# Layer norms of the residual tails: sums and squares of uncentred tiles as they come, then two tiles normed per group, with all low parts of u on one engine

## The chip, the cores and the metric

One core of one Trainium2 chip runs the whole program. The metric is the device time in microseconds, the median over runs. PE is TensorE, DVE VectorE, ACT ScalarE, POOL GpSimd, SP SyncE.

## The reference, cut to what matters

Two transformer blocks over 512 tokens of width 1024, then two layers of another block. Each of the two first layers has three residuals, and each residual ends in a layer norm whose result goes, modulated, into the next product:

```python
def layer_norm(x, g, b):
    mu = jnp.mean(xf, -1, keepdims=True)
    var = jnp.mean(jnp.square(xf - mu), -1, keepdims=True)
    return ((xf - mu) * lax.rsqrt(var + LN_EPS) * g + b)

def deepnorm_residual(x, f, gate, g, b, weight=1.0):
    return layer_norm(DN_ALPHA * x + weight * (1 + gate) * f, g, b)

for l in range(DEPTH):          # DEPTH = 2
    x = deepnorm_residual(x, swiglu(modulate(x, sh1, sc1), ...), g1, ..., 0.5)
    x = deepnorm_residual(x, mixer(modulate(x, sh2, sc2)), g2, ...)
    x = deepnorm_residual(x, swiglu(modulate(x, sh3, sc3), ...), g3, ..., 0.5)
```

## The kernel before

Activations lie transposed, as eight tiles of 128 features by 512 tokens (XA). A product walks over its output tiles m; for each, PE multiplies k = 8 or 11 weight tiles. Each fp32 product is made of three matmuls: high part of the weights by high and low part of the input, low part of the weights by the high part (L560 to L562).

Weights come as slabs of at most 1024 columns through a ring of three raw buffers (SP loads them) and a ring of three split buffers. ACT writes the high part (L481, `act_slabs`), then DVE or POOL the low part (L491, `low_slabs`). The letters of `low_in` and `low_out` name the engine, by the slab's number modulo their count: v is DVE, g is POOL. A slab with k = 8 is one tile of 1024 columns; a tile with k = 11 has two slabs of 768 and 640 columns. A split buffer is free once PE has ended the tile that used it.

Every engine has one queue, in the order in which its program (a generator) emits. `act_linear`, `dve_linear` and `pool_linear` do the same for each m: first the slabs up to `L.ahead(m)` (with one slab a tile: up to tile m + 2; with two: up to both slabs of tile m + 1), then the epilogue of m. `pe_linear` calls `after(m)` behind each tile. So work in an epilogue stands in front of the next slab's split on that engine.

A residual tail (`pe_tail`, `act_tail`, `dve_tail`, `pool_tail`) makes the product in two halves of the tokens: part A (columns 0 to 255, eight tiles), then part B. DVE adds each tile to XA (L841, `v_z`), POOL keeps a running total of the tiles (L902). There are six tails: f00, f01, f10, f11 end a feed-forward product (k = 11), e and o end a mixer's (k = 8). The norm of half A is spread over the groups m = 0 to 4 of part B, that of half B over the first groups of the next product's own A part (`gu` for e, f01 and o; `xa`/`ga` of `pe_rg` for f00 and `oi` of `pe_odd` for f10, both with four A tiles only). f11 has no next product of this kind; its half B is normed behind the tail.

The norm, as groups: m = 0: PE sums the total against ones/1024 to the mean (L623), DVE subtracts it from the eight tiles (L961), ACT squares each into a buffer of its own (L930). m = 1: PE sums the eight squares (L922). m = 2: ACT takes the root from PSUM (L934), DVE the reciprocal (L964), then scales tiles 0 to 3 (L970) and makes uf = a x + b (L979; L975 for f11). m = 3: ACT makes UH, the high part of u, for tiles 0 to 3 (L938), DVE the low parts UL of the even tiles (L954), POOL those of the odd ones (L988), and DVE goes on to tiles 4 to 7. m = 4: the rest. In the four-tile stages (`last=3`) groups 3 and 4 are one. The gu parts also have L765, L767 (ACT), L786 (DVE) and L807 (POOL) for the gated product.

## Time and profile before

| | us |
|---|---|
| median of 3 runs (lowest to highest) | 4399.35 (4396.97 to 4401.84) |
| the profiled execution: its time | 4397.6 |
| its span | 4396.0 |
| PE busy, share of the span | 4028.2, 92% |
| DVE, ACT, POOL busy | 2294.8, 1533.6, 1227.5 |
| idle of PE before L560 that ended with a low part, DVE L491 / POOL L491 | 74.9 / 46.0 |
| idle of PE before L623 that ended with POOL's total L902 | 10.2, 4 times |
| mean granted clock of PE | 0.952 |

Busy time of PE overlaps itself, as matmuls are pipelined; idle time is what is left of a stretch. A row of the timeline gives start and length in us, engine, line, operation, what it writes and reads, its shape and how many were merged, and in brackets the idle time of the engine before it and what ended that. Times run from the start of the span. A granted clock of 1.00 is 2.4 GHz and 0.50 is 1.2 GHz; a value between is a mean over the stretch.

### The profile page before, as it was taken

To read this page: it belongs to the slowest core of one execution; us is meant where nothing else is said; L and a number is where in the kernel's file an instruction comes from. 1 tells how busy PE (TensorE), PEld (TensorE's weight loads), DVE (VectorE), ACT (ScalarE), POOL (GpSimd) and SP (SyncE) were. 2 spreads that over 40 slices of the span, in tenths; PEclk is the share of its full clock that TensorE was granted. 3 is DMA by queue.
4 is the path that set the end of the run, shared out by engine and by line. 5 is a ranking of instruction groups with operands and counts; after the bars stand their busy time and mean duration, and the time that the engine had idled before them with its cause. 6 is when DMAs were issued, how large, how long until landed. Compare 5 with 4: busy or idle time off the path is not lost.

```text
span 4396.0 us, 53914 instructions
## 1 busy us (share of the span) xinstructions
PE 4028.2 (92%) x21044; PEld 3271.2 (74%) x21044; DVE 2294.8 (52%) x3918; ACT 1533.6 (35%) x2626; POOL 1227.5 (28%) x815
## 2 busy tenths in 40 slices
PE   5999768989998998799998899989999989999999
PEld 4888556788888888468887675778868867668777
DVE  5555772565556786445334788421363358630452
ACT  3223433443234224344233223433254232343352
POOL 1114433242024014024013229123202332514214
PEclk9999889989999999899999997999999989999899
DMA  6565233235554554114324110011101111112102
GB/s 256 170 200 165 74 115 123 92 133 174 193 175 144 170 198 140 60 46 142 91 93 126 44 48 26 29 44 59 53 15 32 65 49 57 35 41 89 63 18 93
DMA packets 131596, 433.11 MB, mean 99 GB/s; under 512 B 14480, under 2 KB 14480, under 8 KB 130704
## 3 DMA queue, kind: packets, MB, share of 16 engines
q1 hardware_dynamic: 130912, 427.04, 29.8%
q8 instruction: 169, 2.77, 0.3%
q10 hardware_dynamic: 432, 2.62, 0.2%
q14 instruction: 83, 0.68, 0.0%
HBM read 427.51 MB, written 2.10 MB: 98 GB/s over the span
## 4 chain that ended last, share of the span: by engine, by line
PE 77%; DVE 12%; issue 4%; POOL 3%; ACT 2%; DMA 1%; SPq 0%; DVEq 0%; ACTq 0%; POOLq 0%
PE ps L560 19%; PE ps L561 19%; PE ps L562 19%; PE ps L1584 5%; PE ps L1603 4%; DVE cut L1880 3%; PE ps L1593 2%; POOL cut L491 1%; PE ps L586 1%; PE ps L588 1%; PE ps L587 1%; DVE cut L1097 1%; PE ps L1813 1%; PE ps L922 1%; PE ps L558 1%
## 5 line engine op out<-in xcount | busy, mean ns | idle before, releaser
L560 PE MATMUL ps<-cut 128*128 128x512 f32 (+1 forms) x5216 | 1863.0, 357 | 213.7 <-DVE cut L491 74.9
L561 PE MATMUL ps<-cut 128*128 128x512 f32 (+1 forms) x5216 | 1833.4, 352 | 0.0
L562 PE MATMUL ps<-cut 128*128 128x512 f32 (+1 forms) x5216 | 1831.5, 351 | 0.0
L560 PEld LDWEIGHTS ps<-cut 128*128 128x128 f32 x5216 | 1010.2, 194 | 379.8 <-issue 156.8
L561 PEld LDWEIGHTS ps<-cut 128*128 128x128 f32 x5216 | 1011.8, 194 | 129.0 <-issue 6.3
L562 PEld LDWEIGHTS ps<-cut 128*128 128x128 f32 x5216 | 1009.9, 194 | 125.7
L491 POOL TENSOR_TENSOR cut<-cut 128x1024 fp32r<-128x1024 f32 (+3 forms) x316 | 683.9, 2166 | 1455.8 <-ACT cut L481 1455.7
L481 ACT ACTIVATE cut<-cut 128x1024 fp32r<-128x1024 f32 (+3 forms) x680 | 633.4, 938 | 742.0 <-PE ps L562 627.5
L491 DVE TENSOR_TENSOR cut<-cut 128x1024 fp32r<-128x1024 f32 (+2 forms) x364 | 439.6, 1209 | 454.1 <-ACT cut L481 454.1
L807 POOL TENSOR_TENSOR cut<-cut 128x512 fp32r<-128x512 f32 (+1 forms) x100 | 139.1, 1391 | 1006.5 <-ACT cut L767 1006.4
L1880 DVE SCALAR_TENSOR_TENSOR cut<-cut,cols 128x512 f32<-128x512 f32 (+1 forms) x330 | 282.7, 857 | 11.7
L1584 PE MATMUL ps<-cut 64*128 64x512 f32 (+6 forms) x704 | 270.7, 504 | 8.5 <-DVE cut L1429 6.6
L2010 DVE TENSOR_TENSOR cut<-cut,ps 128x512 f32<-128x512 f32 x72 | 42.3, 596 | 414.1 <-PE ps L562 409.0
L1614 ACT ACTIVATE cut<-cut,st 128x768 f32<-128x768 f32 (+4 forms) x192 | 143.8, 749 | 309.5 <-DVE st L1654 309.5
L1603 PE MATMUL ps<-cut 128*64 128x128 f32 (+1 forms) x1632 | 229.0, 287 | 3.5 <-ACT cut L1624 1.2
L1603 PEld LDWEIGHTS ps<-cut 128*64 128x64 f32 (+1 forms) x1632 | 186.8, 148 | 34.3 <-issue 31.5
L1584 PEld LDWEIGHTS ps<-cut 64*128 64x128 f32 (+1 forms) x704 | 126.2, 203 | 105.8 <-issue 80.3
L767 ACT ACTIVATE cut<-cut 128x512 fp32r<-128x512 f32 (+1 forms) x100 | 58.1, 581 | 405.1 <-DVE cut L786 405.1
L504 DVE CUSTOM_DVE_ANT_0 cut<-cut,cols 128x1024 f32<-128x1024 f32 x128 | 173.1, 1353 | 13.9 <-DMA cut<-in_mod_w 13.3
L786 DVE TENSOR_TENSOR cut<-cut,ps 128x512 f32<-128x512 f32 (+1 forms) x100 | 62.3, 623 | 209.1 <-PE ps L562 208.9
L1593 PEld LDWEIGHTS ps<-const,cut 128*128 128x128 f32 x816 | 92.8, 148 | 84.8 <-issue 54.9
L1593 PE MATMUL ps<-const,cut 128*128 128x128 f32 x816 | 140.4, 301 | 12.6 <-DVE cut L1667 12.2
(255 smaller groups left out, 3709.5 us busy)
## 6 DMA issues: line engine op xcount, KB each, us to landing
cut<-in_ffn_in SPq DMA_DIRECT2D x200, 512.0 KB, 3.9
cut<-in_mod_w SPq DMA_DIRECT2D x128, 512.0 KB, 4.1
cut<-in_ffn_out SPq DMA_DIRECT2D x96, 384.0 KB, 3.2
cut<-in_ffn_out SPq DMA_DIRECT2D x96, 320.0 KB, 3.5
cut<-in_w_ada SPq DMA_DIRECT2D x48, 512.0 KB, 3.5
cut<-in_w_merge SPq DMA_DIRECT2D x48, 512.0 KB, 3.4
cut<-in_even_in SPq DMA_DIRECT2D x36, 512.0 KB, 3.5
cut<-in_proj SPq DMA_DIRECT2D x48, 256.0 KB, 2.6
```

The lines of the kernel that those rows point to most:

```text
L481: se.activation(halves(n)[0], raw(n), ACT.Copy).then_inc(*sig("a_hi", n))
L491: engine.tensor_tensor(lo, raw(n), hi.bitcast(F32), ALU.subtract).then_inc(*sig(which + "_lo", n))
L504: ve.tensor_tensor_reduce(junk, w, cb, 1.0, col("mod_b", 72 * l + i), ALU.mult, ALU.add, modc[:, 72 * l + i:72 * l + i + 1]).then_inc(*sig ...
L560: te.matmul(o, hi[:, k - ka, w], xs[0], start=k == 0, stop=False)
L561: te.matmul(o, hi[:, k - ka, w], xs[1], start=False, stop=False)
L562: ins = te.matmul(o, lo[:, k - ka, w], xs[0], start=False, stop=last)
L807: ge.tensor_tensor(HL[:, t, g[0]:g[1]], FTMP[t % 2][:, g[0]:g[1]], HH[:, t, g[0]:g[1]].bitcast(F32), ALU.subtract).then_inc(*sig("g_hl", g ...
L1584: ins = te.matmul(PS[b][:, 0:w], lh, rh, start=k == 0, stop=k == len(pairs) - 1)
L1593: ins = te.transpose(PS[b][:, (k - b0) * 128:(k - b0 + 1) * 128], sbuf[:, k * 128:(k + 1) * 128], ident)
L1603: ins = te.matmul(PS[b][p0:p1, 0:128], vk, pbuf[:, k * 128:(k + 1) * 128], start=k == 0, stop=k == len(J["v"]) - 1)
L1614: se.activation(sbuf[:, 0:at_], sbuf[:, 0:at_], ACT.Exp, bias=nm, accum_out=sm).then_inc(*sig("a_exp", tag, i))
L1880: ve.scalar_tensor_tensor(out=o, in0=x, scalar=c, in1=o, op0=ALU.mult, op1=ALU.add).then_inc(*sig("v_tap", l, t, h0, j))
```

## The change

Squares are taken of the tiles as they are, not of centred ones. In every tail, ACT squares each tile behind its residual (`act_square`, two buffers TT[0], TT[1]), and PE adds the square of tile m - 1 to one PSUM bank behind tile m (`pe_square`); that bank is kept out of the rotation meanwhile (`kept`). Behind tile 0 of the following part PE adds the eighth square and sums the total. Group 0 of the norm is then, on DVE: copy of the mean, -mean * mean, plus the mean of squares, maximum with 0; ACT's root (now of an SBUF tile); reciprocal, mean times reciprocal. Each group m = 0 to 3 norms the tiles 2m and 2m + 1: times rstd, minus mean * rstd, then uf; ACT makes their UH in the same group. UL of a pair follows in the next group, all on DVE. `pool_ln` is gone. The low parts of the weights go to POOL for two slabs of three (`ggv`) in the A parts of `gu` and `oi` and in the B parts of the tails.

With these letters, the engines of the slabs are (before, after): tail B parts f00 and f10 vgvg..., gvggvg...; f01 vgvg..., ggvggv...; f11 gvgv..., gvggvg...; e vgvgvgvg, gvggvggv; o gvgvgvgv, vggvggvg; next A parts e vgvgvgvg, ggvggvgg; f01 vgvgvgvg, gvggvggv; o gvgvgvgv, gvggvggv; f10 vgvg, vggv; f00 gggg in both.

```diff
@@ -89,11 +89,11 @@
 def low_in(name):
-    return {"A": "vg", "B": "vg"}.get(name[-1], "v")
+    return {"A": "ggv", "B": "vg"}.get(name[-1], "v")
 def low_out(name):
-    return {"A": "v", "B": "vg"}.get(name[-1], "v")
+    return {"A": "v", "B": "ggv"}.get(name[-1], "v")
 def weight_plan():
...
@@ -520,9 +520,11 @@
-    bank_until, turn, bank = [None] * 8, [0], {}
+    bank_until, turn, bank, kept = [None] * 8, [0], {}, set()
     def pe_take(until):
+        while turn[0] % 8 in kept:
+            turn[0] += 1
         b = turn[0] % 8
         turn[0] += 1
         if bank_until[b] is not None:
...
@@ -721,7 +723,7 @@
     def u_ready(u, h):
         def ready(k, gi):
-            return [("g_u", u, k)] if u == "start" else [(("v_ul", "g_u")[k % 2], u, h, k)]
+            return [("g_u", u, k)] if u == "start" else [("v_ul", u, h, k)]
         return ready
     def hl_of(l, f, half, tile):
...
@@ -844,22 +844,26 @@
     def pe_tail(name, x, ready, tag, nxt):
         for part in ab(*name):
-            after = (lambda m: pe_ln(tag, "A", m)) if part[-1] == "B" else None
-            yield from pe_linear(part, x, [HALF[part[-1]]], lambda m, gi: ("v_z", part, m),
-                                 ready if part[-1] == "A" else none, after)
+            h = part[-1]
+            def after(m):
+                if h == "B" and m == 0:
+                    yield from pe_ln(tag, "A")
+                if m:
+                    yield from pe_square(tag, h, m - 1)
+            yield from pe_linear(part, x, [HALF[h]], lambda m, gi: ("v_z", part, m), ready if h == "A" else none, after)
         if not nxt:
-            yield from pe_ln(tag, "B", 0)
-            yield from pe_ln(tag, "B", 1)
+            yield from pe_ln(tag, "B")
     def act_tail(name, tag, nxt):
         for part in ab(*name):
             def epilogue(m):
+                yield from act_square(part, tag, m)
                 if part[-1] == "B":
                     yield from act_ln(tag, "A", m)
             yield from act_linear(part, epilogue)
         if not nxt:
-            for m in range(3):
-                yield from act_ln(tag, "B", m)
+            yield from act_ln(tag, "B", 0)
     def dve_tail(name, l, j, tag, nxt):
         lng, lnb = col("ln_g", 8 * (3 * l + j), 8), col("ln_b", 8 * (3 * l + j), 8)
...
@@ -901,54 +905,59 @@
                         ge.wait_ge(*(yield "g_total", tag, part[-1], m - 1))
                     ge.tensor_tensor(total, total if m > 1 else XA[:, 0, g[0]:g[1]], XA[:, m, g[0]:g[1]],
                                      ALU.add).then_inc(*sig("g_total", tag, part[-1], m))
-                if part[-1] == "B" and nxt:
-                    yield from pool_ln(tag, "A", m)
             yield from pool_linear(part, epilogue)
-    def sq_at(tag, h, t):
-        o = {("A", "e"): 44544, ("A", "o"): 44544, ("B", "f00"): F0, ("B", "f11"): 44544}.get((h, tag), 42496 if h == "A" else 46592)
-        return ar(o + 256 * t, o + 256 * t + 256)
-    def pe_ln(tag, h, m):
+    def square(h, t):
+        return TT[t % 2][:, HALF[h][0]:HALF[h][1]]
+    def pe_square(tag, h, t):
+        if t == 0 and tag == "f00" and h == "A":
+            te.wait_ge(*(yield "d_const",))
+        if t == 0:
+            b = bank["p_var", tag, h] = yield from pe_take(("v_var", tag, h))
+            kept.add(b)
+        te.wait_ge(*(yield "a_sq", tag, h, t))
+        te.matmul(PS[bank["p_var", tag, h]][:, 0:256], ones, square(h, t), start=t == 0, stop=t == NT - 1).then_inc(*sig("p_var", tag, h, t))
+    def act_square(part, tag, t):
+        h, g = part[-1], HALF[part[-1]]
+        se.wait_ge(*(yield "v_z", part, t))
+        if t >= 2:
+            se.wait_ge(*(yield "p_var", tag, h, t - 2))
+        se.activation(square(h, t), XA[:, t, g[0]:g[1]], ACT.Square).then_inc(*sig("a_sq", tag, h, t))
+    def pe_ln(tag, h):
+        total = TOTAL[:, HALF[h][0]:HALF[h][1]]
+        yield from pe_square(tag, h, NT - 1)
+        yield from pe_sum([(total, ("g_total", tag, h, 7))], ones, 256, ("v_mean", tag, h), ("p_mean", tag, h))
+        kept.discard(bank["p_var", tag, h])
+    def uf(h, t):
+        return TT[(3, 4, 0, 1)[t % 4]][:, HALF[h][0]:HALF[h][1]]
+    def act_ln(tag, h, m):
         g = HALF[h]
         if m == 0:
-            if tag == "f00" and h == "A":
-                te.wait_ge(*(yield "d_const",))
-            yield from pe_sum([(TOTAL[:, g[0]:g[1]], ("g_total", tag, h, 7))], ones, 256, ("v_cen", tag, h, 7), ("p_mean", tag, h))
-        if m == 1:
-            b = bank["p_var", tag, h] = yield from pe_take(("a_std", tag, h))
-            for t in range(NT):
-                te.wait_ge(*(yield "a_sq", tag, h, t))
-                te.matmul(PS[b][:, 0:256], ones, sq_at(tag, h, t), start=t == 0, stop=t == NT - 1).then_inc(*sig("p_var", tag, h, t))
-    def act_ln(tag, h, m, last=4):
+            rstd = TT[2][:, g[0]:g[1]]
+            se.wait_ge(*(yield "v_var", tag, h))
+            se.activation(rstd, rstd, ACT.Sqrt, bias=epsc(LN_EPS), scale=1.0).then_inc(*sig("a_std", tag, h))
+        for t in (2 * m, 2 * m + 1) if m < 4 and tag != "f11" else ():
+            se.wait_ge(*(yield "v_nrm", tag, h, t))
+            se.activation(UH[:, t, g[0]:g[1]], XA[:, t, g[0]:g[1]], ACT.Identity, bias=deriv[:, 16 + t:17 + t],
+                          scale=deriv[:, 8 + t:9 + t]).then_inc(*sig("a_uh", tag, h, t))
+    def dve_ln(tag, h, m, last=4):
         g, rstd = HALF[h], TT[2][:, HALF[h][0]:HALF[h][1]]
-        if m == 0:
-            for t in range(NT):
-                se.wait_ge(*(yield "v_cen", tag, h, t))
-                se.activation(sq_at(tag, h, t), XA[:, t, g[0]:g[1]], ACT.Square).then_inc(*sig("a_sq", tag, h, t))
-        if m == 2:
-            se.wait_ge(*(yield "v_eps", 2))
-            se.wait_ge(*(yield "p_var", tag, h, NT - 1))
-            se.activation(rstd, PS[bank["p_var", tag, h]][:, 0:256], ACT.Sqrt, bias=epsc(LN_EPS), scale=1.0).then_inc(*sig("a_std", tag, h))
-        if tag != "f11" and m in (3, last):
-            for t in range(4 * m - 12, 4 * m - 8 if last == 4 else NT):
-                se.wait_ge(*(yield "v_nrm", tag, h, t))
-                se.activation(UH[:, t, g[0]:g[1]], XA[:, t, g[0]:g[1]], ACT.Identity, bias=deriv[:, 16 + t:17 + t],
-                              scale=deriv[:, 8 + t:9 + t]).then_inc(*sig("a_uh", tag, h, t))
-    def uf(h, t):
-        return TT[(3, 4, 0, 1)[t % 4]][:, HALF[h][0]:HALF[h][1]]
-    def dve_ln(tag, h, m, last=4):
-        g, rstd = HALF[h], TT[2][:, HALF[h][0]:HALF[h][1]]
+        mr = (TT[4] if tag == "f11" else FTMP[2])[:, g[0]:g[1]]
         ca, cbb = [deriv[:, 8 * i:8 * i + 8] for i in (1, 2)]
-        def lows(tiles_):
-            for t in tiles_:
+        def lows(t0):
+            for t in (t0, t0 + 1) if tag != "f11" else ():
                 ve.wait_ge(*(yield "v_uf", tag, h, t))
                 ve.wait_ge(*(yield "a_uh", tag, h, t))
                 ve.tensor_tensor(UL[:, t, g[0]:g[1]], uf(h, t), UH[:, t, g[0]:g[1]].bitcast(F32),
...
@@ -956,36 +965,41 @@
         if m == 0:
             ve.wait_ge(*(yield "p_mean", tag, h))
-            for t in range(NT):
-                x = XA[:, t, g[0]:g[1]]
-                ve.tensor_tensor(x, x, PS[bank["p_mean", tag, h]][:, 0:256], ALU.subtract).then_inc(*sig("v_cen", tag, h, t))
-        if m == 2:
+            mean, sq = PS[bank["p_mean", tag, h]][:, 0:256], PS[bank["p_var", tag, h]][:, 0:256]
+            ve.tensor_copy(mr, mean).then_inc(*sig("v_mean", tag, h))
+            ve.wait_ge(*prev("v"))
+            ve.scalar_tensor_tensor(out=rstd, in0=mr, scalar=-1.0, in1=mr, op0=ALU.mult, op1=ALU.mult).then_inc(*sig("v_msq", tag, h))
+            ve.wait_ge(*prev("v"))
+            ve.tensor_tensor(rstd, sq, rstd, ALU.add).then_inc(*sig("v_sqm", tag, h))
+            ve.wait_ge(*prev("v"))
+            ve.tensor_scalar(rstd, rstd, 0.0, None, ALU.max).then_inc(*sig("v_var", tag, h))
             ve.wait_ge(*(yield "a_std", tag, h))
             ve.reciprocal(rstd, rstd).then_inc(*sig("v_rstd", tag, h))
             ve.wait_ge(*prev("v"))
-        if m == 3 and tag != "f11":
-            yield from lows((0, 2))
-        for t in {2: (0, 1, 2, 3), 3: (4, 5, 6, 7)}.get(m, ()):
+            ve.tensor_tensor(mr, mr, rstd, ALU.mult).then_inc(*sig("v_mr", tag, h))
+        elif m <= last:
+            yield from lows(2 * m - 2)
+        for t in (2 * m, 2 * m + 1) if m < 4 else ():
             x = XA[:, t, g[0]:g[1]]
-            ve.tensor_tensor(x, x, rstd, ALU.mult).then_inc(*sig("v_nrm", tag, h, t))
-        for t in {2: (0, 1, 2, 3), 3: (4, 5, 6, 7)}.get(m, ()):
+            if t == 0:
+                ve.wait_ge(*(yield "a_sq", tag, h, 7))
+            ve.tensor_tensor(x, x, rstd, ALU.mult).then_inc(*sig("v_cen", tag, h, t))
+        for t in (2 * m, 2 * m + 1) if m < 4 else ():
+            x = XA[:, t, g[0]:g[1]]
+            ve.wait_ge(*(yield "v_mr", tag, h))
+            ve.wait_ge(*(yield "v_cen", tag, h, t))
+            ve.tensor_tensor(x, x, mr, ALU.subtract).then_inc(*sig("v_nrm", tag, h, t))
+        for t in (2 * m, 2 * m + 1) if m < 4 else ():
             x = XA[:, t, g[0]:g[1]]
             ve.wait_ge(*(yield "v_nrm", tag, h, t))
             if tag == "f11":
                 ve.tensor_scalar(x, x, deriv[:, 24 + t:25 + t], deriv[:, 32 + t:33 + t], ALU.mult, ALU.add).then_inc(*sig("v_x", tag, h, t))
             else:
                 if t >= 4:
-                    ve.wait_ge(*(yield ("v_ul", "g_u")[t % 2], tag, h, t - 4))
+                    ve.wait_ge(*(yield "v_ul", tag, h, t - 4))
                 ve.tensor_scalar(uf(h, t), x, ca[:, t:t + 1], cbb[:, t:t + 1], ALU.mult, ALU.add).then_inc(*sig("v_uf", tag, h, t))
-        if m == last and tag != "f11":
-            yield from lows((4, 6))
-    def pool_ln(tag, h, m, last=4):
-        for t in ({3: (1, 3, 5, 7)} if last == 3 else {3: (1, 3), 4: (5, 7)}).get(m, ()):
-            g = HALF[h]
-            ge.wait_ge(*(yield "a_uh", tag, h, t))
-            ge.wait_ge(*(yield "v_uf", tag, h, t))
-            ge.tensor_tensor(UL[:, t, g[0]:g[1]], uf(h, t), UH[:, t, g[0]:g[1]].bitcast(F32), ALU.subtract).then_inc(*sig("g_u", tag, h, t))
+        if m == 3 and last == 3:
+            yield from lows(6)
     def dve_scale_x(tag, t):
         for h in "AB":
...
```

What is left out are the callers: `pe_ln(u, "B")` behind the first A tile only, `act_ln` without `last`, `nothing` in place of `pool_ln`, five groups of `dve_ln` for f11, and the new semaphore names.

## Rows read from the trace of the kernel before

**Rows 1.** Windows view: start:end, length, PE busy (count), granted clock, DMA share, GB/s.
```profile
391.80:432.80 41.00, 34.41 (x249) 0.96 0.44 132
432.80:459.90 27.10, 20.83 (x140) 0.89 0.45 166
897.76:920.80 23.04, 23.04 (x193) 1.00 0.52 172
920.80:952.60 31.80, 26.80 (x189) 0.89 0.34 112
952.60:989.30 36.70, 30.04 (x214) 0.86 0.37 124
1306.80:1347.70 40.90, 34.32 (x251) 0.96 0.43 133
1347.70:1386.30 38.60, 29.40 (x213) 0.91 0.37 122
1703.40:1745.50 42.10, 35.54 (x251) 0.92 0.41 129
1745.50:1777.10 31.60, 23.03 (x140) 0.81 0.33 110
1970.40:2000.50 30.10, 25.95 (x187) 0.94 0.34 107
2000.50:2037.10 36.60, 31.39 (x217) 0.91 0.41 144
```

**Rows 2.** Timeline of the first product after f01, the norm of half B.
```profile
1353.16 0.67 PE L623 MATMUL ps<-cut,const 128*128 128x256 f32 x2 [2.56 <-POOL cut L902]
1353.87 2.74 DVE L961 TENSOR_TENSOR cut<-cut,ps 128x256 f32<-128x256 f32 x8 [1.43 <-PE ps L623]
...
1364.76 0.47 ACT L934 ACTIVATE cut<-ps,small 128x256 f32<-128x256 f32 x1
...
1365.27 1.75 DVE L964 RECIPROCAL cut<-cut 128x256 f32<-128x256 f32 x1 [3.74 <-ACT cut L934]
1366.25 2.40 POOL L491 TENSOR_TENSOR cut<-cut 128x1024 fp32r<-128x1024 f32 x1 [4.13 <-ACT cut L481]
1367.05 2.90 DVE L970 TENSOR_TENSOR cut<-cut 128x256 f32<-128x256 f32 x4
1369.87 1.37 DVE L979 TENSOR_SCALAR cut<-cut,deriv 128x256 f32<-128x256 f32 x4
...
1371.93 2.06 ACT L938 ACTIVATE cut<-cut,deriv 128x256 fp32r<-128x256 f32 x4
...
1377.18 1.21 DVE L491 TENSOR_TENSOR cut<-cut 128x1024 fp32r<-128x1024 f32 x1
...
1378.53 0.55 PE L560 MATMUL ps<-cut 128*128 128x256 f32 x1 [6.62 <-DVE cut L491]
```

**Rows 3.** Timeline of tail f00's B part, DVE beside POOL.
```profile
413.34 0.74 DVE L954 TENSOR_TENSOR cut<-cut 128x256 fp32r<-128x256 f32 x2
413.50 2.52 POOL L902 TENSOR_TENSOR cut<-cut 128x256 f32<-128x256 f32 x1 [2.46 <-DVE cut L841]
414.01 1.42 DVE L970 TENSOR_TENSOR cut<-cut 128x256 f32<-128x256 f32 x4
415.35 0.81 DVE L979 TENSOR_SCALAR cut<-cut,deriv 128x256 f32<-128x256 f32 x1
```

**Rows 4.** Groups by form: line, operation, count, busy us, mean ns, idle before.
```profile
L481 ACT ACTIVATE cut<-cut 128x1024 fp32r<-128x1024 f32 x424 | 445.2, 1053 | 366.7 <-PE ps L562 298.7 <-PE ps L588 41.8 <-DMA cut<-in_ffn_in 8.4
...
L841 DVE SCALAR_TENSOR_TENSOR cut<-ps,deriv,cut 128x256 f32<-128x256 f32 x96 | 46.0, 479 | 64.0 <-PE ps L562 63.9
```

**Rows 5.** The chain of work that ended last, one piece: start us, us, what.
```profile
958.79 3.45 PE ps L922 x16
```

**Rows 6.** Timeline of ACT at a root with one wait, L1838.
```profile
3121.42 1.28 ACT L1838 ACT_TABLE_LOAD   x1
3124.59 0.69 ACT L1838 ACTIVATE cut<-ps,small 128x512 f32<-128x512 f32 x1 [1.89 <-PE ps L623]
```

More of the change, by code:

```diff
@@ L210 @@
     "v_recip": ("v_rstd", "v_grs", "v_crs", "v_rr", "v_hr", "v_wr", "v_cr"),
-    "v_norm": ("v_cn", "v_rn", "v_hn", "v_wn", "v_cn2", "v_cd"),
+    "v_norm": ("v_mean", "v_sqm", "v_msq", "v_var", "v_mr", "v_cn", "v_rn", "v_hn", "v_wn", "v_cn2", "v_cd"),
     "v_rope": ("v_rp0", "v_rp1", "v_rp"),
@@ L744, in pe_ffn @@
                 ready = none if half or i == 2 else u_ready(u, gu[-1])
-                after = (lambda m: pe_ln(u, "B", m)) if gu[-1] == "A" else None
+                after = (lambda m: pe_ln(u, "B") if m == 0 else nothing(m)) if gu[-1] == "A" else None
                 yield from pe_linear(gu, urhs, [g], lambda m, gi: (("a_sil", "v_hid")[m % 2], gu, m), ready, after)
@@ L808, in epilogue @@
                                          ALU.subtract).then_inc(*sig("g_hl", gu, m // 2))
-                    if gu[-1] == "A":
-                        yield from pool_ln(u, "B", m)
                 yield from pool_linear(gu, epilogue)
@@ L888, in dve_tail @@
         if not nxt:
-            for m in range(4):
+            for m in range(5):
                 yield from dve_ln(tag, "B", m)
@@ L1003, in pe_rg @@
                     ready = u_ready(u, x) if (t, i) == (0, 0) else none
-                    after = (lambda _: pe_ln(u, "B", 2 * t + i)) if x == "A" else None
+                    after = (lambda _: pe_ln(u, "B")) if (x, t, i) == ("A", 0, 0) else None
                     yield from pe_linear((kind, t, x), urhs, [HALF[x]], lambda m, gi: (("a_xp", "a_gelu")[i], t), ready, after,
@@ L1070, in act_rg @@
                 if x == "A":
-                    yield from act_ln("f00", "B", 2 * t, 3)
+                    yield from act_ln("f00", "B", 2 * t)
                 yield from act_linear(("ga", t, x), nothing)
                 if x == "A":
-                    yield from act_ln("f00", "B", 2 * t + 1, 3)
+                    yield from act_ln("f00", "B", 2 * t + 1)
         yield from gates(1)
@@ L1149, in pool_rg @@
                 for i, kind in enumerate(("xa", "ga")):
-                    yield from pool_linear((kind, t, x), lambda _: pool_ln("f00", "B", 2 * t + i, 3) if x == "A" else nothing(_))
+                    yield from pool_linear((kind, t, x), nothing)
         for t in range(2, NT + 1):
@@ L1450, in pe_odd @@
         for name in ab("oi"):
-            after = (lambda m: pe_ln(u, "B", m)) if name[-1] == "A" else None
+            after = (lambda m: pe_ln(u, "B") if m == 0 else nothing(m)) if name[-1] == "A" else None
             yield from pe_linear(name, urhs, [HALF[name[-1]]], lambda m, gi: ("a_cq", m, name[-1]), u_ready(u, name[-1]), after)
@@ L1480, in epilogue @@
                 if name[-1] == "A":
-                    yield from act_ln("f10", "B", m, 3)
+                    yield from act_ln("f10", "B", m)
             yield from act_linear(name, epilogue)
@@ L1554, in pool_odd @@
     def pool_odd():
-        yield from pool_linear(("oi", "A"), lambda m: pool_ln("f10", "B", m, 3))
+        yield from pool_linear(("oi", "A"), nothing)
         for name in (("oi", "B"), ("qn",), ("qp",), ("kn",), ("vu",)):
```

## The prediction

> **What bounds the kernel now.** I read the granted clock and PE's busy time over the stages with a residual tail first, then what PE waited for there, then the order of the instructions on DVE, ACT and POOL in one such stage. Zero of a stage is the end of a weight tile. A half-width tile (256 columns) of eight k steps takes 23.04 / 8 = 2.88 us of PE, back to back [rows 1]; one of eleven k steps takes 11/8 of that, 3.96 us. Elsewhere PE is nearly always full; in the ten stretches around the norms it is not: length minus busy is 6.6, 6.3, 5.0, 6.7, 6.6, 9.2, 6.6, 8.6, 4.2 and 5.2 us, 65 us together, and the granted clock is 0.81 to 0.96 in them against 1.00 in a stretch before [rows 1]. So the norms cost PE time only where a later weight tile isn't split in time. What ends PE's waits is the low part of a weight slab (L491) on DVE, once 6.6 us, and once the running total on POOL, 2.6 us [rows 2]. DVE is late because its queue holds the norm: it waits 3.74 us for the root, takes 1.75 us for the reciprocal, and then the multiplies and the low parts before the slab's turn comes [rows 2].
>
> **Prices, from rows.** Reciprocal 1.75, root 0.47; four tensor_tensor of 256 columns 1.42, so 0.36 each in a run, the same for a tensor_scalar (1.37 for four), two low parts 0.74; four uh activations 2.06, 0.5 each; the low part of a 1024-column slab 2.40 on POOL and 1.21 on DVE [rows 2, 3], its high part on ACT 1.05 [rows 4]. Eight square-sum matmuls take 3.45, 0.43 each [rows 5]. From the mean's matmul to DVE's first use pass 0.7 [rows 2]. The added small operations aren't in the trace as they stand: the copy of the mean from PSUM and the sum with PSUM I take at 0.4 (the centring with PSUM runs at 2.74 / 8 = 0.34 [rows 2]), -m*m at 0.48 (the residual's scalar_tensor_tensor [rows 4]), the maximum at 0.36. Bounds for the four: 1.3 and 3 us.
>
> **DVE and POOL exclude each other.** While POOL worked on a slab from 1366.25 to 1368.65, four DVE multiplies that began at 1367.05 took 2.90 instead of 1.42 [rows 2, 3]: the first waited until POOL was done. The other way round POOL's 256-column add took 2.52 instead of some 0.73: it waited until the run of DVE tensor_tensor was over and got in ahead of the tensor_scalar (0.81 instead of 0.4) [rows 3]. So low parts that move from DVE to POOL don't relieve DVE; they hold it up for 2.4 instead of 1.2 us.
> The Trainium skill (SBUF — State Buffer, section Who interferes with whom) has this as an exclusive lock, taken by whoever issues first for one whole instruction. The trace agrees with the lock, not with one instruction as the turn: POOL waited through six. By the page's turn POOL's slab would be ready some 1.4 us sooner in about five stages, and the sum below 7 us smaller.
>
> **What the change does, part by part.**
> (1) Squares come with the tiles. Seven of eight square matmuls of the A half move into the A part, where PE is full: 7 x 0.43 x 6 tails = +18.1 us. For the B half they move from the next product into the B part, where A's went away. The price of a full engine, no cover.
> (2) ACT now squares each tile after v_z. Behind it on ACT are the next slabs' high parts. In an eleven-k tail, z is at 2.1 us after a tile (0.74 high and 0.83 low of the 640-column slab, scaled from the 1024-column rows with 0.1 for the start, and 0.48 [rows 4]), the square ends at 2.5, the next high part at 3.4, its low part on DVE at 4.3, and PE wants it at 3.96 + 0.43 = 4.4. Nothing lost in A parts; in B parts with POOL on both slabs some 0.7 a tile, counted below.
> (3) The norm's group 0 now does all of mean, root, reciprocal and two tiles in one go. After tile 0: last square and mean matmul 0.9, DVE starts at 1.25; copy, -m*m, sum, maximum with their waits 1.9, so v_var at 3.1; root seen by DVE at 3.7; reciprocal to 5.45; mean times rstd 5.9; two multiplies 6.6, two subtracts 7.3, two uf 8.0. ACT waits in its queue for each: uh of the second tile ends at 8.1. **The next slab's high part stands behind that** (act_linear splits up to two tiles ahead before its epilogue): 9.15, its low part 10.4 on DVE or 11.6 on POOL at best. PE has work until 0.9 + 2 x 2.88 = 6.7 (eight-k tiles), or 0.9 + 3.96 + 0.43 = 5.3 (eleven-k). So every stage but the last one has a stall of 3.7 to 5.5 us right there. Before, ACT only squared eight tiles in 2.7 us here and uh lagged DVE's multiply by a group.
> (4) Groups 1 to 3 repeat it: each has on DVE two low parts, two multiplies, two subtracts, two uf (2.9 us, before the even low parts alone and no subtracts), and one slab. With the exclusion a group lasts 2.9 + 2.4 (POOL) or + 1.2 (DVE), plus 0.4 to 1.2 for v_hid, z and the totals: about 5.3 us for a tile that PE does in 2.9 to 4.4.
>
> Walked through instruction by instruction with these prices and the slabs' new engines:
> - eleven-k B part, tails f00, f01, f10. Work 7 x 3.96 + 8 x 0.43 + 0.43 = 31.6; tiles 2, 3, 4 start 4.7, 2.7, 2.6 late, the rest 0.7: 10.7. Plus 1.7 for the clock (the least that a row shows, 0.96 over 41 us): 44.0 against 41.0, 40.9, 42.1 [rows 1]: +8.0.
> - eight-k B part, tails e, o. Slab 3 waits for POOL until 13.0, tiles 4 to 6 are 0.6, 2.3, 3.5 late; tile 7 ends at 35.4 (o: 34.4). With clock 37.1 and 36.1 against 31.8 and 30.1: +11.3.
> - next product's A part, norm B (e, f01, o). Work 21.1 after tile 0; tile 3 6.3 late, tile 5 4.6, the rest 1.3: 33.3 after it, and 2.88 + 33.3 + 1.7 = 37.9 against 36.7, 38.6, 36.6: +1.8. PE's seven squares that left are in it, and so is f01's total, which no longer stands behind the second slab (2.6 [rows 2]; that slab is DVE's now).
> - f00 and f10, where only four tiles cover norm B. The last low part of B is ready at some 24 us after tile 0, and PE needs it to end the first B tile: 31.0 and 31.2 against 27.1 and 31.6 [rows 1]: +3.5. Nothing is hidden here, and the squares that left PE bring nothing.
> - f11: no uh and no low parts, so ACT isn't held; its B part -0.5. After it one chain: before, 4.4 to the reciprocal and 1.75 + 16 x 0.36; now 2.5 and 1.75 + 0.45 + 24 x 0.36: +1.3. Together +0.8.
> Sum 8.0 + 11.3 + 1.8 + 3.5 + 18.1 + 0.8 = +43.5. The profiled execution took 4397.6 (span 4396.0 and 1.6 around it), so 4441; the median of the runs is 1.75 above it: **4443 us**.
>
> **A table load that isn't in it.** Where an activation with a new function has one wait, the load ran during it: a load of 1.28 at 3121.42, and then ACT sat 1.89 us for PE before the root at 3124.59 [rows 6]. The new root has one wait, on v_var, and I count the load as hidden. If it isn't, +1.3 in nine stages, 12 us.
> The Trainium skill (ScalarE: Activation LUTs, section What ACT_TABLE_LOAD costs) gives 2.66 us a switch, its drain included. The row shows 1.28; by the page's figure, unhidden, it would be 24 us.
>
> **Rivals.**
> (a) More of the same: table loads in the chain and deeper clock dips (0.81 to 0.89 as in four rows [rows 1], 2 us more in six stages): +43.5 + 12 + 12 = +68, 4467. Chance 0.12.
> (b) DVE and POOL overlap better than the turn that I took; each walk loses its waits for the other engine (3.2 us in three stages, 3.4 in two, 4 in three, 5 in two: 38 us): +5.5, 4405, within what a run can tell. For: only two places show who goes first. Against: both engines' sums of work don't shrink. Chance 0.10.
> (c) Faster: group 0 ends before PE runs out, so that ACT's split isn't late, and the groups keep to PE's pace. That needs uh 1 to end at 4.2 instead of 8.1. With 3 us of waiting left a stage: eleven-k 34.6 + 1.7 (-15), eight-k B -8, next A -27, f00/f10 -12, +18 for the squares: -44, 4355. For: the pass over eight centred tiles and their squares does go; from the first centring to the reciprocal it was 11.4 us (1353.87 to 1365.27 [rows 2]), now 2.5. Half of it gives 4380. Against: the chain is a sum of durations from rows, and the reciprocal and four multiplies alone are 3.2. Chance 0.16.
> (d) Forecast: 0.62.
>
> **Numbers.** A measurement tells about 0.2%, 8.8 us: faster is below 4390.6, slower above 4408.1. Faster 0.16 (c), same 0.10 (b), slower 0.74 (a and forecast). The range takes in (b), (a) and the milder half of (c), and leaves out about 0.08 on either side: 4380 to 4478. The likeliest case's own range is 4420 to 4465.
>
> **What would show it.** Right: PE waits of 4 to 6 us for the slab two or three tiles after each mean; ACT's high part beginning just after the second uh of each group; DVE multiplies and subtracts of 1.5 to 2.6 us beside L491 on POOL; A parts 3 us longer. Step (3) is wrong if slab 3's high part begins within 5 us of the mean, step (4) if the groups follow each other in less than 4 us, (1) if the A parts keep their length. The forecast falls if PE's waiting in the ten stretches is under 65 us in sum instead of over 100.

## The result, and the profile after

The changed kernel takes 4433.35 us, the median of 4 runs (4431.55 to 4436.74), against 4398.16 us (4392.74 to 4401.84, 4 runs) before: a ratio of 1.0082, 95% interval 1.0064 to 1.0099. That is 35 us more where 43.5 more were forecast. The profiled execution took 4436.74, its span is 4435.4, 39.4 over that of before.

PE's waits of the changed kernel, largest first: what PE waited for, us in total, times, longest us. L562 is the old L560, L625 the old L623.

```profile
PE ps L562 <- POOL cut L491: 89.5, 30, 11.6
PE ps L562 <- DVE cut L491: 60.2, 11, 32.7
...
PE ps L923 <- ACT cut L930: 9.5, 4, 3.6
...
PE ps L625 <- POOL cut L906: 4.7, 4, 2.2
```

Waits for POOL's low parts rose from 46.0 us to 89.5, those for DVE's fell from 74.9 to 60.2, those for POOL's total from 10.2 to 4.7. Together PE waits 28.8 us more for low parts. The longest of each kind lie outside the norms and are the same in both kernels: 32.6 us for DVE before the first product (32.7 in the changed kernel) and 11.6 us for POOL.

The same stretches as in [rows 1], each from the end of a tile to the end of a tile, in the windows view of the changed kernel (start:end, length, PE busy, granted clock, DMA share, GB/s). Shown are f00's B part and what follows, the same of e, and the B parts of f01 and o; the sum holds all ten and a stretch of 23.04 at full PE.

```profile
396.20:442.90 46.70, 36.73 (x250) 0.89 0.39 115
442.90:472.80 29.90, 19.52 (x130) 0.85 0.40 148
...
937.20:969.30 32.10, 25.58 (x185) 0.95 0.28 100
969.30:1009.50 40.20, 29.45 (x200) 0.83 0.34 118
1329.90:1376.70 46.80, 35.45 (x248) 0.89 0.35 113
...
2007.20:2042.80 35.60, 28.29 (x186) 0.86 0.28 99
...
sum 405.24, PE 310.80; mean PE 28.25
```

| stretch | before [rows 1] | after | forecast |
|---|---|---|---|
| B part f00, f01, f10 | 41.0, 40.9, 42.1 | 46.7, 46.8, 44.6 | 44.0 each |
| B part e, o | 31.8, 30.1 | 32.1, 35.6 | 37.1, 36.1 |
| next part f00, f10 | 27.1, 31.6 | 29.9, 29.6 | 31.0, 31.2 |
| next part e, f01, o | 36.7, 38.6, 36.6 | 40.2, 39.8, 36.9 | 37.9 each |
| length minus PE busy, the ten | 65 | 94 (382.2 - 287.8) | over 100 |

The five B parts grew by 19.9 us (forecast 19.3), the five next parts by 5.8 (forecast 5.3). DVE's residual marks each tile of f00's A part (timeline, start us, us):

```profile
370.93 0.48 DVE L841 SCALAR_TENSOR_TENSOR cut<-ps,deriv,cut 128x256 f32<-128x256 f32 x1
375.31 0.48 DVE L841 SCALAR_TENSOR_TENSOR cut<-ps,deriv,cut 128x256 f32<-128x256 f32 x1
```

The tiles are 4.37 us apart instead of 3.96. Between the end of one norm and the first tile of the next B part the changed kernel falls behind by 4.4, 3.5, 2.9, 3.0, 3.3 and 1.8 us in the six tails, 18.9 together (forecast 18.1).

Group 0 of f00's half A, from the timelines of PE, DVE, ACT and POOL:

```profile
397.24 0.42 DVE L969 COPY cut<-ps 128x256 f32<-128x256 f32 x1 [0.38 <-PE ps L625]
397.25 1.57 POOL L491 TENSOR_TENSOR cut<-cut 128x640 fp32r<-128x640 f32 x1 [0.86 <-ACT cut L481]
397.50 1.28 ACT L947 ACT_TABLE_LOAD   x1
397.69 1.41 DVE L971 SCALAR_TENSOR_TENSOR cut<-cut 128x256 f32<-128x256 f32 x1
399.92 0.51 ACT L947 ACTIVATE cut<-cut,small 128x256 f32<-128x256 f32 x1 [1.14 <-DVE cut L975]
400.47 1.75 DVE L977 RECIPROCAL cut<-cut 128x256 f32<-128x256 f32 x1 [0.58 <-ACT cut L947]
403.72 1.09 ACT L950 ACTIVATE cut<-cut,deriv 128x256 fp32r<-128x256 f32 x2 [3.29 <-DVE cut L991]
404.72 1.46 ACT L481 ACTIVATE cut<-cut 128x768 fp32r<-128x768 f32 x2
405.58 0.96 DVE L491 TENSOR_TENSOR cut<-cut 128x768 fp32r<-128x768 f32 x1 [0.91 <-ACT cut L481]
406.69 0.55 PE L562 MATMUL ps<-cut 128*128 128x256 f32 x1 [5.11 <-DVE cut L491]
```

Tile 0 ended at 396.2. The reciprocal ends 6.0 us after that (402.22), the second UH 8.6 us after it (404.81), and ACT makes the next slab's high part right behind; PE goes on at 406.69, after 5.11 us idle.

### The profile page after: what moved, and what is told of

Its sections match the earlier page's. It is cut to its first block, busy times and chain, and to the rows that moved or that the text cites. A ratio compares the mean times of both kernels' runs of the same rounds, so it can differ in the third digit from the quotient of the medians.

```text
span 4435.4 us, 54130 instructions
## 1 busy us (share of the span) xinstructions
PE 4032.5 (91%) x21044; PEld 3272.5 (74%) x21044; DVE 2336.0 (53%) x4000; ACT 1537.2 (35%) x2626; POOL 1208.1 (27%) x793
## 4 chain that ended last, share of the span: by engine, by line
PE 76%; DVE 14%; issue 3%; ACT 3%; POOL 2%; DMA 1%; SPq 0%; DVEq 0%; ACTq 0%; POOLq 0%
PE ps L562 19%; PE ps L563 19%; PE ps L564 19%; PE ps L1598 5%; PE ps L1617 4%; DVE cut L1894 3%; PE ps L1607 2%; POOL cut L491 2%; PE ps L588 1%; PE ps L589 1%; PE ps L590 1%; DVE cut L1111 1%; PE ps L1827 1%; PE ps L560 1%; ACT cut L481 1%
## 5 line engine op out<-in xcount | busy, mean ns | idle before, releaser
L562 PE MATMUL ps<-cut 128*128 128x512 f32 (+1 forms) x5216 | 1876.3, 360 | 239.0 <-POOL cut L491 89.5
L562 PEld LDWEIGHTS ps<-cut 128*128 128x128 f32 x5216 | 1015.4, 195 | 412.5 <-issue 187.2
L491 POOL TENSOR_TENSOR cut<-cut 128x1024 fp32r<-128x1024 f32 (+3 forms) x334 | 731.4, 2192 | 1516.3 <-ACT cut L481 1515.9
L491 DVE TENSOR_TENSOR cut<-cut 128x1024 fp32r<-128x1024 f32 (+2 forms) x346 | 408.5, 1182 | 477.4 <-ACT cut L481 477.4
```

The costliest lines, as they stand in the source:

```text
L491: engine.tensor_tensor(lo, raw(n), hi.bitcast(F32), ALU.subtract).then_inc(*sig(which + "_lo", n))
L562: te.matmul(o, hi[:, k - ka, w], xs[0], start=k == 0, stop=False)
```

## The experiments

Two causes were to be told apart. **Q, ACT's queue:** the high part of the next slab stands behind the square and behind UH of the same group, which ends the whole chain on DVE. **L, the letters:** two slabs of three go to POOL (2.4 us each, and DVE held meanwhile). `ggv`/`vg` in the names below are the letters. The kernel before, run beside them, had medians of 4396.9 to 4398.7.

**e1: the changed kernel with the old letters.**

```diff
-    return {"A": "ggv", "B": "vg"}.get(name[-1], "v")
+    return {"A": "vg", "B": "vg"}.get(name[-1], "v")
-    return {"A": "v", "B": "ggv"}.get(name[-1], "v")
+    return {"A": "v", "B": "vg"}.get(name[-1], "v")
```

> The changed kernel with the letters of low_in and low_out as before (vg), all else as changed. Theory Q (the loss sits in the order of ACT's queue: the next slab's high part stands behind the uh of the same group): the slab's low part is late whoever makes it, so this stays within 8 us of the changed kernel, 4425 to 4441. Theory L (the loss is the larger share of POOL's slow low parts, which also hold DVE up): 10 to 20 us faster than the changed kernel, 4413 to 4423.

4416.49 us, ratio 1.0044 (1.0031 to 1.0056). The letters cost 17 us of the 35, as L expected. The edit puts back three things at once: POOL's longer slabs, the holding up of DVE by them, and where DVE's own slabs fall; no run separates these.

**e2: the kernel before with the new letters** (the same edit the other way round).

> The kernel before with the new letters (ggv) alone. Theory Q: within 6 us of before. Theory L: 15 to 25 us slower than before, since the norm there also has POOL's odd low parts of u and both engines exclude each other.

4405.47 us, 1.0015 (1.0006 to 1.0024): +6.8, just over Q's 6 and well under L's 15 to 25. In the old norm the letters cost less than half of what they cost in the new one. That this is so because DVE has more to do beside POOL there is my reading; no run shows it.

**e3: the changed kernel with the square matmuls of tiles 0 and 7 only.**

```diff
-        te.matmul(... square(h, t), start=t == 0, stop=t == NT - 1)...
+        if t in (0, NT - 1):
+            te.matmul(... square(h, t), start=t == 0, stop=t == NT - 1)...
```

> The changed kernel without the square matmuls of tiles 1 to 6 on PE (their squares are missing from the variance, so the output isn't the reference's); ACT squares all tiles as before. Both theories: the A parts of the six tails are full on PE and lose 6 x 0.43 = 2.6 us each, 15.5 in all. In B parts and behind them Q and L say that PE waits anyway, so at most a few us more: 4413 to 4418. If the B parts gain as much, 4402.

4432.6 us, 1.0078 (1.0065 to 1.009): nothing came back that the median can tell, where 15.5 were expected. In f00's A part:

```profile
378.44 0.48 DVE L841 SCALAR_TENSOR_TENSOR cut<-ps,deriv,cut 128x256 f32<-128x256 f32 x1
382.67 0.48 DVE L841 SCALAR_TENSOR_TENSOR cut<-ps,deriv,cut 128x256 f32<-128x256 f32 x1
...
381.24 0.36 PE L562 MATMUL ps<-cut 128*128 128x256 f32 x1 [0.18 <-DVE cut L491]
```

The tiles are still 4.23 to 4.37 us apart, and PE now waits for low parts. So PE's 0.43 a tile was covered by a second limit of the same size: residual, then ACT's square, then the next high part, then its low part. By itself this run doesn't say that PE's squares are free; e10 takes the other limit away first. The trace shows a second loss beside it: e's A part does get shorter (22.9 us from its first residual to the B part's first, instead of 25.6), but e's B part then takes 3.1 us longer (35.2 from residual to residual instead of 32.1), with one wait of 5.66 us for POOL's low part. Up to f11's last tile the trace is 4.4 us ahead of the changed kernel.

**e4: in the groups that carry the norm, ACT splits one more slab ahead of the norm's instructions** (behind the square).

```diff
                 yield from act_square(part, tag, m)
                 if part[-1] == "B":
+                    yield from act_slabs(LIN[part].ahead(m) + 1)
                     yield from act_ln(tag, "A", m)
```

and the same ahead of `act_ln(u, "B", m)` and in the stages behind f00 and f10.

> The changed kernel, but in every group of the norm ACT splits one more slab ahead before it waits for the norm (its release is the tile that has just ended). Q: slab 3's high part is ready 1.1 us after tile 0 instead of 8 to 9, POOL's low part 3.5 after it, so the stalls of 5 us in group 0 shrink where POOL has the slab, by 2 to 4 us a stage in eleven stages, and later groups too: 20 to 40 us faster, 4393 to 4413. L: the engines' work and their exclusion are the same, so less than 10 us faster.

4413.27 us, 1.0033 (1.002 to 1.0045): 20 us of the 35 came back. Nothing was taken from any engine, only ACT's order changed.

**e6: as e4, but in the tails the slab is split ahead of the square too**, in A and B parts.

> As e4_split_first, but the slab is split before the square of the tile, and in the A parts too. With one square, eleven-k A parts kept their 4.3 us a tile, so there the square on ACT in front of the next high part may set the pace, not PE's 0.43. If so, this pays nothing alone, since PE's square alone makes 4.4 of it: equal to e4 within 4 us, 4409 to 4417. If ACT's order costs more than that in B parts: 4403 to 4409.

4406.0 us, 1.0021 (1.0012 to 1.0029): another 7 by the medians, 5 by the ratios; the intervals of e4 and e6 overlap, so this second step is not clear of the noise. Both steps together are: ACT's order was worth 27 us. f00's A part still goes at 4.37 us a tile.

**e5: the changed kernel with the reciprocal replaced** by a `tensor_scalar` that writes 0.5.

> The changed kernel with the reciprocal of 1.75 us in group 0 replaced by a tensor_scalar that writes a constant (the norm isn't divided by the deviation, so the output isn't the reference's). It shortens group 0 by 1.4 us in twelve norms and leaves the rest. Theory Q (a chain that PE waits for): 11 x 1.4 = 15 us faster than the changed kernel, 4418. Theory L (DVE and POOL are full through their exclusion): the reciprocal has one input and didn't exclude POOL, so less than 6 us, 4428 or more.

4424.45 us, 1.0063 (1.005 to 1.0075): -9. The kernel has 12 such halves, each 1.46 shorter, 17.5 us in all; so by the medians about half of a shortening of the chain arrives, but the interval overlaps that of the changed kernel. In the trace 13.0 us of the 16.1 that lie ahead of f11's last tile are there. It lies between what Q and L expected and decides for neither.

**e7: e6 with the old letters.**

> e6_split_before_square with the letters vg as before. If Q and L act on different waits, 17 and 20 us add up: 4396. If both shorten the same waits, 4404 to 4410.

4391.23 us, 0.9987 (0.9979 to 0.9996). The two gains add up (27 + 17 = 44, measured 42), a little better than either expectation, and the kernel is now 6 us faster than before. f00's group 0 in its timeline (L932 is the square, L952 UH), and then the rows of its waits view for low parts:

```profile
396.63 0.85 ACT L481 ACTIVATE cut<-cut 128x768 fp32r<-128x768 f32 x1 [0.16 <-DMA cut<-in_ffn_out]
397.38 0.40 ACT L932 ACTIVATE cut<-cut 128x256 f32<-128x256 f32 x1
403.02 1.09 ACT L952 ACTIVATE cut<-cut,deriv 128x256 fp32r<-128x256 f32 x2 [3.29 <-DVE cut L993]
403.89 0.95 DVE L491 TENSOR_TENSOR cut<-cut 128x768 fp32r<-128x768 f32 x1
404.98 0.35 PE L562 MATMUL ps<-cut 128*128 128x256 f32 x1 [4.10 <-DVE cut L491]
```

```profile
PE ps L562 <- DVE cut L491: 69.6, 19, 32.7
PE ps L562 <- POOL cut L491: 37.8, 10, 11.3
```

The 768-column slab's high part is there at 397.5, 8 us sooner, and PE still waits 4.10: its low part is DVE's and stands behind the chain in DVE's queue. But the later groups are short now. B parts, from DVE's residual of tile 0 to that of tile 7, where 41.1, 40.9 and 42.2 stood before for f00, f01 and f10, take 40.1, 39.9 and 41.1. Those of e and o don't gain: 33.0 and 33.7, where 31.8 and 30.9 stood, and the A parts still pay for their squares. So in the stages e7 only breaks even. Its residual of f11's last tile is 1.8 us later than that of the kernel before (2396.87), and what makes it faster in the end lies behind it, in the norm of f11's half B and after:

```profile
2398.64 0.48 DVE L842 SCALAR_TENSOR_TENSOR cut<-ps,deriv,cut 128x256 f32<-128x256 f32 x1 [2.32 <-PE ps L564]
```

**e8: e7 with DVE making that low part ahead of its norm instructions.**

```diff
                 if part[-1] == "B":
+                    yield from low_slabs("v", ve, LIN[part].ahead(m) + 1)
                     yield from dve_ln(tag, "A", m)
```

> e7_both, and DVE too makes its low part of that slab before the norm's group (tails and gu only). The slab is ready 2.3 us after the tile instead of 9 to 10, at the price of a group 0 that starts 1 to 2 us later. Q: 5 to 15 us faster than e7. Rival: the later chain gives it back, within 4 us of e7.

4408.83 us, 1.0027 (1.0016 to 1.0037): 18 worse. DVE and PE of e8 in the same place, and then its waits:

```profile
396.85 1.45 DVE L491 TENSOR_TENSOR cut<-cut 128x768 fp32r<-128x768 f32 x1 [1.33 <-ACT cut L481]
398.22 0.41 DVE L973 COPY cut<-ps 128x256 f32<-128x256 f32 x1
407.10 0.58 PE L562 MATMUL ps<-cut 128*128 128x256 f32 x1 [4.71 <-POOL cut L491]
```

```profile
PE ps L562 <- POOL cut L491: 74.0, 24, 11.6
PE ps L562 <- DVE cut L491: 44.3, 7, 32.7
```

Waits for DVE fell by 25 us and those for POOL rose by 36. The copy of the mean begins 3.2 us after the residual of tile 0 (395.03) instead of 0.9 (395.67 in e7), so UH comes later, and with it the high part that stands behind UH on ACT and that POOL needs. What helps on ACT, which mostly waits in the chain, hurts on DVE, which makes it.

**e9: the kernel before with e4's edit** in its own norm groups.

> The kernel before, with one edit of the reordering alone: in the parts whose groups carry the norm, ACT makes the high part of one more slab ahead of the norm's instructions of that group. Theory Q (the new norm's groups, which put UH of the same group ahead of the next high part, are what makes ACT's order costly; the kernel before has UH one group behind its multiply and so little to gain): within 9 us of before, 4390 to 4400, and the wait of 6.6 us for DVE's low part behind the norm B of f01 stays. Rival (the reordering is a gain in any norm, and what the mended new kernel won has nothing to do with the new norm): 4370 to 4385, at least 12 us under before.

4405.29 us, 1.0018 (1.0009 to 1.0027): 7 us slower, so no gain at all, and the rival falls. The wait behind f01's norm B stays, as expected; it is 7.30 us here. PE's waits for DVE's low parts rose from 74.9 us to 84.2. So the order is worth something in the new norm only. The likely reason is that UH waits there for the chain of its own group, while before it lagged a group.

**e10: e7 with the square matmuls of tiles 0 and 7 only** (e3's edit).

> The changed kernel with the next high part split ahead of the square and the norm on ACT and with the old letters of the slabs' low parts (the 4391 us kernel), and without the square matmuls of tiles 1 to 6 in every tail half: the variance is then that of two tiles, a part of the sum is left out. Theory P (with ACT's order mended, PE's 0.43 us a square is the price of a full engine again): 36 matmuls in A parts x 0.43 = 15.5 us less than the 4391 kernel, 4376, and eleven-k A parts at 3.96 us a tile. Rival (A parts go by ACT or DVE even so, as when the squares alone were dropped): within 4 us of 4391 and a tile still at 4.2 us or more.

4377.8 us, 0.9958 (0.9946 to 0.9971): 13.4 less than e7 (13 by the ratios), where 36 x 0.43 = 15.5 were expected. The letters don't matter for this: DVE makes the low parts of all the slabs of the tails' A parts in either kernel, so what differs from e3 there is ACT's order alone. f00's A part goes at 3.96 us a tile again:

```profile
378.61 0.48 DVE L842 SCALAR_TENSOR_TENSOR cut<-ps,deriv,cut 128x256 f32<-128x256 f32 x1
382.57 0.48 DVE L842 SCALAR_TENSOR_TENSOR cut<-ps,deriv,cut 128x256 f32<-128x256 f32 x1
```

**e11: e7 with the reciprocal replaced** (e5's edit).

> The same mended kernel (4391 us), complete but for the reciprocal of the norm of the tails, which is replaced by a tensor_scalar that writes a constant, 1.75 to about 0.4 us in eleven halves: a part of the computation is left out. Theory (once ACT's split no longer stands behind the chain of group 0, the chain's length is hidden by the slabs that are ready): within 4 us of 4391. Rival (the chain still decides, as DVE's own low parts stand behind it): 9 to 15 us less, 4376 to 4382.

4372.06 us, 0.9948 (0.9935 to 0.9962): 19 less than e7 (17 by the ratios). The theory fell, and the rival's 9 to 15 was too small: with 12 halves, not the 11 that I wrote, it is 17.5 us of chain, and all of it arrives. In e7 DVE's next low part stands behind the chain, so each us of the chain is one of PE's. In f00's B part the wait of 4.10 us is shorter by the full 1.46 (PE waits another 0.96 at the next tile, at 408.61):

```profile
403.04 0.35 PE L562 MATMUL ps<-cut 128*128 128x256 f32 x1 [2.64 <-DVE cut L491]
```

**e12: e7 without the maximum with 0.**

> The mended kernel (high part split ahead of the square and the norm on ACT, old letters, 4391.23 us), and DVE's maximum of the variance with 0 dropped from group 0; the reference has no such step, and the mean of squares minus the squared mean of 1024 values of order one stays far above it. Theory (the chain of group 0 on DVE sets the end of each norm stage, at its full length): 11 halves x 0.4 us and their wait = 4.4 to 5.6 us less, 4386 to 4387, 0.27% under the kernel before. Rival (only the reciprocal's place after the root counts, what stands ahead of the root is hidden): within 2 us of 4391.

4388.29 us, 0.9978 (0.9969 to 0.9987): 3 less than e7 (4 by the ratios), between the two expectations, and the intervals of e7 and e12 overlap: this run doesn't tell them apart. It has the lowest median of the versions that leave nothing of the reference out, 10 us under the kernel before.

## Why the prediction was right, and where it wasn't

**The sum.** Forecast +43.5 in the stages; they gave +19.9, +5.8 and +18.9, and f11's B part and end 5.3 and -5.7 or so, 44 together: at the norm behind L1838 the changed kernel is 43.9 us late (3168.53 instead of 3124.59 [rows 6]):

```profile
3168.53 0.69 ACT L1852 ACTIVATE cut<-ps,small 128x512 f32<-128x512 f32 x1 [1.89 <-PE ps L625]
```

By the end it is 39.4 late in the span and 35 in the median, though the code behind that point is the same. From the last residual of f11 on, before took 1999.1 us in its profile, but e2 and e9, which have the same norm, 1995.1 and 1994.6. The runs of one kernel lie 5 to 15 us apart, so I put these 4 to 9 us down to that; no run shows it.

**Step (1), squares in A parts at 0.43 on full PE:** right in size (18.1 forecast, 18.9 measured, 4.37 us a tile), and e10 gave 13.4 of 15.5 back. But it wasn't the only limit: e3 gave nothing back in the median.

**Step (2), nothing lost to ACT's order in A parts:** right only because PE hid it. My own walk had the slab ready at 4.3 us and PE wanting it at 4.4; e3 shows the 4.3 in the tiles' spacing. Dropping one of two limits that lie 0.1 us apart tells nothing of either.

**Step (3), group 0:** right, and e4 and e6 show ACT's queue as a cause (Q). Behind the end of tile 0 the forecast had DVE's start at 1.25, the reciprocal's end at 5.45, that of the second UH at 8.1, DVE's low part ready at 10.4, a stall of 3.7 to 5.5; f00 shows 1.0, 6.0, 8.6, 10.3 and 5.11. The half us is DVE's -m*m, 1.41 instead of the 0.48 that I took, because POOL was on a slab; over the 12 halves it took 0.98 in the mean, 6 us that the sum didn't have. Over the other ten stretches the waits there are 3.6 to 6.5 us, but for e's B part, where they fall apart into 1.79 and 2.60. The table load was hidden, as forecast: it ran while ACT waited for v_var.

**Step (4), groups that last 5.3 us:** right in the mean, and only there. From one group's first multiply (L986) to the next one's it is 5.1 us over the thirty of the ten stretches, but 2.7 to 7.9 one by one, and eleven are under the 4 us that the forecast named as the sign of its being wrong. The stages' sums came right (five next parts +5.8); e's B part didn't. It was to take 37.1 and took 32.1, the largest miss of a stage: I had tiles 4 to 6 late by 6.4 us together, and there PE waited 2.13 in all (at 959.52). That f00's and f01's 2.7 and 2.8 more cancelled it was luck: in e3 the same B part of e took 3.1 us longer, though its edit leaves ACT, DVE and POOL their order. A wait that no step had is PE's for ACT's square: 9.5 us in four places, 1.79 of it in e. In o, where it is longest (3.58), the square waits for DVE's residual, and ahead of the residual stands a low part whose high part came behind UH:

```profile
2017.36 0.42 ACT L930 ACTIVATE cut<-cut 128x256 f32<-128x256 f32 x1 [1.69 <-DVE cut L841]
```

The stall and the exclusion as they look in the gu part behind e (L1000 is the step to uf):

```profile
981.19 1.04 ACT L481 ACTIVATE cut<-cut 128x1024 fp32r<-128x1024 f32 x1
982.31 3.38 POOL L491 TENSOR_TENSOR cut<-cut 128x1024 fp32r<-128x1024 f32 x1 [8.48 <-ACT cut L481]
983.39 3.18 DVE L1000 TENSOR_SCALAR cut<-cut,deriv 128x256 f32<-128x256 f32 x2
985.83 0.55 PE L562 MATMUL ps<-cut 128*128 128x256 f32 x1 [5.45 <-POOL cut L491]
```

POOL takes 3.38 instead of 2.40 [rows 2] because DVE's run comes first, then DVE takes 3.18 for two steps that last 0.73 alone.

**f11 was wrong twice.** Its B part was to gain 0.5, since ACT makes no UH; it lost 5.3. ACT isn't held, but DVE's chain of group 0 stands in front of DVE's own slab, and PE waited for it:

```profile
2414.75 0.55 PE L562 MATMUL ps<-cut 128*128 128x256 f32 x1 [5.30 <-DVE cut L491]
```

The end was to lose 1.3; from that residual to the norm behind L1838 it gained 5.7. From DVE's residual of the last tile to the start of the reciprocal it was 12.4 us before (2396.87 to 2409.26) and is 7.8 now. First the kernel before, then the changed one:

```profile
2402.45 2.74 DVE L961 TENSOR_TENSOR cut<-cut,ps 128x256 f32<-128x256 f32 x8 [5.10 <-PE ps L623]
2403.47 5.18 PE L922 MATMUL ps<-cut,const 128*128 128x256 f32 x16 [1.05 <-ACT cut L930]
2409.26 1.75 DVE L964 RECIPROCAL cut<-cut 128x256 f32<-128x256 f32 x1 [4.07 <-ACT cut L934]
```

```profile
2446.50 0.48 DVE L841 SCALAR_TENSOR_TENSOR cut<-ps,deriv,cut 128x256 f32<-128x256 f32 x1 [4.66 <-PE ps L564]
2450.86 1.19 PE L625 MATMUL ps<-cut,const 128*128 128x256 f32 x2 [2.19 <-POOL cut L906]
2454.34 1.75 DVE L977 RECIPROCAL cut<-cut 128x256 f32<-128x256 f32 x1 [0.58 <-ACT cut L947]
```

The term that was mis-sized is the old chain. I gave it 4.4 us from DVE's first use of the mean to the reciprocal (the stretch that is 2.5 in rival (c)), and it took 6.8 (2402.45 to 2409.26), since the sum of the eight squares, 3.45 in [rows 5], took 5.18 there, at a granted clock of 0.71. The new one took 2.25 (2452.09 to 2454.34) where I had 2.5. Behind the reciprocal the eight subtractions and the added multiply cost 3.0, where the sum has 3.3. That leaves 1.5 us of gain at the norm's last instruction, and 5.7 were measured. What I had left out is that the next norm's sums start from the first finished tiles. They begin 12.5 us behind the residual now (at 2459.03) instead of 16.7 (at 2413.61): the reciprocal comes 4.6 us sooner, and as tiles are finished two at a time, the first ones don't wait for the later tiles' added steps. So PE takes up the next product 3.0 us sooner, counted from the residual. Before and changed kernel:

```profile
2437.22 0.77 PE L560 MATMUL ps<-cut 128*128 128x512 f32 x1 [14.39 <-POOL cut L1763]
```

```profile
2483.87 0.77 PE L562 MATMUL ps<-cut 128*128 128x512 f32 x1 [14.74 <-POOL cut L1777]
```

Another 1.5 come in the first full product, where the granted clock was 0.88 (2450.8 to 2465.0) and is 1.00 now (2497.5 to 2509.0); why is open, and so are the last 1.2. The misses at f11's two places, 5.8 and -7.0, cancel; that is luck.

**The rivals.** (a) Deeper clock dips: the granted clock did fall in eight of the ten stretches, to 0.83 to 0.89, but it rose in e's B part and behind f10, no table load lengthened the chain, and the sum has no room for 24 us more. (b) Better overlap: excluded by the lengths and by 94 us of waiting. (c) Faster: it wanted group 0 over before PE runs out, so that ACT's split isn't late. The change doesn't meet it: the second UH ends at 8.6, not 4.2. In e6 ACT's split isn't late any more, and the kernel is still 9 us slower than before; with the old letters as well (e7) it is 6 us faster and not 44, since DVE's low part still stands behind the chain (e11).

**The letters** I had counted only as longer POOL slabs within the walks. They cost 17 us of the 35; what the walks got right is the sum of both causes, not their shares. That UL of the odd tiles moved from POOL to DVE was never run by itself, so its share is unknown.

## What to carry to other kernels

When a chain of small dependent steps moves into one group, look on each in-order engine for what is queued behind the step that waits for the chain's end: here a reordering on ACT, which is busy a third of the time, brought back 27 of 35 us without any saved work. Move such work ahead on the engine that only waits, not on the one that makes the chain. And an experiment that removes one of two nearly equal limits can show nothing until the other is gone (within 1 us in e3, 13 in e10).

## What the runs showed of the hardware

DVE is held by POOL's slab in more forms than I had counted: a `tensor_scalar` with one input in SBUF (3.18 instead of 0.73 for two) and a `scalar_tensor_tensor` with both inputs there (1.41 instead of 0.42). The residual, whose one input lies in PSUM, isn't; in the changed kernel it runs at its usual 0.48 in the middle of POOL's slab, and the next instruction, with two inputs in SBUF, waits:

```profile
406.25 1.69 POOL L491 TENSOR_TENSOR cut<-cut 128x640 fp32r<-128x640 f32 x1 [7.44 <-ACT cut L481]
406.46 0.48 DVE L841 SCALAR_TENSOR_TENSOR cut<-ps,deriv,cut 128x256 f32<-128x256 f32 x1
406.85 2.25 DVE L963 TENSOR_TENSOR cut<-cut 128x256 fp32r<-128x256 f32 x2
```

The Trainium skill (SBUF — State Buffer, section Who interferes with whom) says that a DVE instruction with two inputs in SBUF contends with GpSimd, one with a single SBUF input only in its two-port modes, which `tensor_scalar` can enter. The trace agrees on the two inputs (2.25 instead of 0.76 for the two instructions here) and on the residual. The `tensor_scalar` was held, as the Trainium skill allows; that it ran in a two-port mode no row shows.
